# Decay exponents with their column part as the bias of ScalarE, and a norm per group in two steps, in a fused forward pass of two blocks

## What is computed

```
a_cs = cumsum(dt * A)                      # inside a block of 128 tokens
Wd   = CB * where(tri, exp(a_cs[l] - a_cs[s]), 0)
y_diag = Wd @ (x * dt)                     # dt of token s
y    = y_fwd + y_bwd + d_skip * x
y    = y * silu(z)
yg   = yg * rsqrt(mean(yg * yg) + eps)     # a group: 4 heads, 256 channels
```

## Time and profile before

| | |
|---|---|
| median of 3 runs | 2742.26 us (2741.68 to 2743.11) |
| profiled execution | 2741.83 us, its span 2739.7 us |
| busy share of the span | PE 97%, PEld 79%, DVE 53%, ACT 42%, POOL 5% |
| DMA | 225.5 MB, mean 82 GB/s |
| granted TensorE clock, mean | 0.983 |
| stage of the change | about 1390 to 1965 us of the span |

### The profile page before, as it was taken

How to read it: one execution, slowest core, us unless ns; L and a number is a source line. 1 busy time by engine, 2 the same in 40 slices (tenths; PEclk the granted TensorE clock), 3 DMA queues, 4 the chain that set the end, 5 groups by cost and what they waited for, 6 DMA issues and landing times.

```text
span 2739.7 us, 32829 instructions
## 1 busy us (share of the span) xinstructions
PE 2650.5 (97%) x13058; PEld 2171.1 (79%) x13058; DVE 1452.2 (53%) x2317; ACT 1141.4 (42%) x1888; POOL 143.8 (5%) x144
## 2 busy tenths in 40 slices
PE   7999999999899999999899999999989999999998
PEld 5888778888676778888678998888867887788886
DVE  5554453433556454333568776675565356443343
ACT  5253443322456543322464655554244334442232
POOL 1110000000100010000001010000000000000000
PEclk9999999999999999999989999999989999999999
DMA  4212223742222123233222121112211243222321
GB/s 138 66 56 69 69 77 100 137 131 95 92 76 83 62 73 105 93 93 107 66 76 68 52 68 54 47 62 77 80 39 39 67 142 108 77 93 93 100 100 62
DMA packets 201112, 225.52 MB, mean 82 GB/s; under 512 B 25152, under 2 KB 133984, under 8 KB 200704
## 3 DMA queue, kind: packets, MB, share of 16 engines
q1 hardware_dynamic: 200960, 223.43, 27.1%
HBM read 213.96 MB, written 9.44 MB: 82 GB/s over the span
## 4 chain that ended last, share of the span: by engine, by line
PE 87%; DVE 6%; ACT 4%; issue 2%; DMA 0%; POOL 0%; SPq 0%; DVEq 0%; POOLq 0%; ACTq 0%
PE bank L1771 22%; PE bank L1773 22%; PE bank L1772 22%; PE bank L1777 2%; PE bank L1778 2%; PE bank L1779 2%; PE bank L1789 2%; PE bank L1985 1%; PE bank L1806 1%; PE bank L1966 1%; PE bank L1950 1%; PE bank L1949 1%; ACT whi L2032 1%; PE bank L1940 1%; PE bank L1922 1%
## 5 line engine op out<-in xcount | busy, mean ns | idle before, releaser
L2240 DVE TENSOR_TENSOR wlo<-raw,whi 128x1024 fp32r<-128x1024 f32 (+1 forms) x389 | 488.6, 1261 | 739.0 <-ACT whi L2032 736.8
L2032 ACT ACTIVATE whi<-raw 128x1024 fp32r<-128x1024 f32 (+1 forms) x389 | 406.9, 1053 | 662.7 <-PE bank L1773 621.3
L1771 PE MATMUL bank<-XAh,whi 128*128 128x512 f32 x1536 | 620.8, 404 | 19.0 <-DVE XAl L2248 10.9
L1772 PE MATMUL bank<-XAl,whi 128*128 128x512 f32 x1536 | 605.3, 394 | 0.0
L1773 PE MATMUL bank<-XAh,wlo 128*128 128x512 f32 x1536 | 604.9, 394 | 0.0
L1771 PEld LDWEIGHTS bank<-XAh,whi 128*128 128x128 f32 x1536 | 292.7, 191 | 97.1 <-issue 31.6
L1773 PEld LDWEIGHTS bank<-XAh,wlo 128*128 128x128 f32 x1536 | 292.3, 190 | 63.1
L1772 PEld LDWEIGHTS bank<-XAl,whi 128*128 128x128 f32 x1536 | 292.9, 191 | 58.9 <-issue 0.7
L1771 PE MATMUL bank<-XBh,whi 128*128 128x512 f32 x816 | 324.8, 398 | 1.7 <-DVE XBl L2246 1.7
L1773 PE MATMUL bank<-XBh,wlo 128*128 128x512 f32 x816 | 318.1, 390 | 0.0
L1772 PE MATMUL bank<-XBl,whi 128*128 128x512 f32 x816 | 317.8, 389 | 0.0
(11 more groups left out here) (331 smaller groups left out, 3599.6 us busy)
## 6 DMA issues: line engine op xcount, KB each, us to landing
raw<-in_w_in SPq DMA_DIRECT2D x68, 512.0 KB, 3.7
raw<-in_up SPq DMA_DIRECT2D x64, 512.0 KB, 3.7
raw<-in_down SPq DMA_DIRECT2D x64, 512.0 KB, 3.7
raw<-in_a_w_in SPq DMA_DIRECT2D x32, 512.0 KB, 4.1
raw<-in_w_up SPq DMA_DIRECT2D x32, 512.0 KB, 3.6
raw<-in_w_down SPq DMA_DIRECT2D x32, 512.0 KB, 3.2
raw<-in_w_kv SPq DMA_DIRECT2D x16, 512.0 KB, 3.5
raw<-in_w_ssd_branch SPq DMA_DIRECT2D x16, 512.0 KB, 3.4
```

Source lines behind the costliest of these rows:

```text
L1771: pe.matmul(out, wh[:, w, c], xh[:, x, 0:s.ntok], start=st, stop=False)
L1772: pe.matmul(out, wh[:, w, c], xl[:, x, 0:s.ntok], start=False, stop=False)
L2032: act.activation(s.hi, s.raw, ACT.Copy).then_inc(s.whi[0], 1)
L2240: dve.tensor_tensor(s.lo, s.raw, s.hi.bitcast(F32), ALU.subtract).then_inc(s.wlo[0], 1)
```

## The change

- sc_arg: the eight matmuls L1940 of a head are gone; the two L1938 stay.
- sc_exp: the Relu of a direction becomes four, one for each token block of 128 columns, whose bias is a column of a new tile K.room (128 partitions x 256): 80 + cs - ln dt, for that block, direction and head. The Exp stays.
- dt_chain: the two dt_rows steps and the two row_parts for rowT[2], rowT[3] are gone, with their distances of two pieces each. L2448, a DVE tensor_tensor, becomes one scalar_tensor_tensor that writes K.room. rowT has 2 tensors, not 4.
- sc_norm now ends with the four Squares; one of the two waits for them on ACT's own queue is gone. A new step sc_scale, one piece later, has the table load, Ln, Exp and the four scalings. sc_back comes four pieces after that.

```diff
-            for d in range(2):
-                yield from p.spaced(2)
...
-                s3 = add("dt_rows", bank=b, ln=t0, d=d, rows=s2.rows, mm=sig("dt.rowmm"))
-                last = split_rows(rowT[2 + d], b, s3.mm, t1, t2, last)
...
-            s7 = add("sc_norm", Y=Y.t, q=q, ss=ss, gated=gates[1], zn=sig("sc.zn"))
+            s7 = add("sc_norm", Y=Y.t, q=q, ss=ss, gated=gates[1], before=ready.get("zn", NONE), means=sig("sc.means"))
...
-            q.free(s7.zn)
+            q.free(s7.means)
+            yield
+            yield from p.spaced(1)
+            s7 = add("sc_scale", Y=Y.t, ss=ss, means=s7.means, zn=sig("sc.zn"))
+            ready["zn"] = s7.zn
             yield
             yield from p.spaced(4)
...
-                pe.matmul(b.t[:, :], one, s.rowT[d][:, :], start=True, stop=False)
-                for c in range(4):
-                    m = pe.matmul(b.t[:, c * P:(c + 1) * P], s.rowT[2 + d][:, c * P:(c + 1) * P], one, start=False, stop=c == 3)
-                m.then_inc(s.arg[d][0], 1)
+                pe.matmul(b.t[:, :], one, s.rowT[d][:, :], start=True, stop=True).then_inc(s.arg[d][0], 1)
...
-                act.activation(s.E.t[:, d, :], s.banks[d].t[:, :], ACT.Relu, scale=-1.0, bias=cap).then_inc(s.below[d][0], 1)
+                for c in range(4):
+                    x, n = slice(c * P, (c + 1) * P), c * 64 + 32 * d + s.hd
+                    m = act.activation(s.E.t[:, d, x], s.banks[d].t[:, x], ACT.Relu, scale=-1.0, bias=K.room[:, n:n + 1])
+                m.then_inc(s.below[d][0], 1)
...
-            dve.tensor_tensor(s.ln.t[:, 0:256], s.ln.t[:, 0:256], cs, ALU.subtract).then_inc(s.rows[0], 1)
+            dve.scalar_tensor_tensor(out=K.room[:, :], in0=cs, scalar=CAP, in1=s.ln.t[:, 0:256], op0=ALU.add, op1=ALU.subtract).then_inc(s.cols[0], 1)
```

More of the change, by code:

```diff
@@ L1193, in make_plan @@
         ss = sb("sst", [P, 8], scope=sc)
-        rowT = [sb(f"rowT{i}", [96, S], F32R, scope=sc) for i in range(4)]
-        K.cap = sb("cap", [P, 1], scope=sc)
+        rowT = [sb(f"rowT{i}", [96, S], F32R, scope=sc) for i in range(2)]
+        K.cap, K.room = sb("cap", [P, 1], scope=sc), sb("room", [P, 256], scope=sc)
         pick = K.pick = sb("pick", [96, 32], F32R, scope=sc)
@@ L1211, in dt_chain @@
             s2 = add("dt_sums", dts=dts, banks=bs, adt_done=s1.adt_done, ln=t0, sums=sig("dt.sums"), ln_in=sig("dt.lnin"), ln_out=sig("dt.lnout"),
-                     cum=sig("dt.cum"), tail=sig("dt.tail"), exps=sig("dt.exps"), done=sig("dt.done"), rows=sig("dt.rows"))
+                     cum=sig("dt.cum"), tail=sig("dt.tail"), exps=sig("dt.exps"), done=sig("dt.done"), cols=sig("dt.cols"))
             bs[0].free(s2.tail)
@@ L1219, in dt_chain @@
             yield
-            for d in range(2):
-                yield from p.spaced(2)
-                while not three.room(1):
-                    yield WAIT
-                b = three.take()
-                s3 = add("dt_rows", bank=b, ln=t0, d=d, rows=s2.rows, mm=sig("dt.rowmm"))
-                last = split_rows(rowT[2 + d], b, s3.mm, t1, t2, last)
-                yield
-            e0.free(last)
+            e0.free(last, s2.cols)
             e1.free(last)
-            ready["dt"], ready["rows"] = s2.done, last
+            ready["dt"], ready["rows"], ready["cols"] = s2.done, last, s2.cols
         def split_rows(dst, bank, mm, t1, t2, before=NONE):
@@ L1375, in outputs @@
                     s = add("sc_arg", banks=bs, rowT=rowT, hd=4 * g + r_, rows=ready["rows"], arg=[sig("sc.arg"), sig("sc.arg")])
-                    s = add("sc_exp", banks=bs, E=E, arg=s.arg, below=[sig("sc.below"), sig("sc.below")], exp=[sig("sc.exp"), sig("sc.exp")])
+                    s = add("sc_exp", banks=bs, E=E, hd=4 * g + r_, cols=ready["cols"], arg=s.arg, below=[sig("sc.below"), sig("sc.below")], exp=[sig("sc.exp"), sig("sc.exp")])
                     for b, v in zip(bs, s.below):
@@ L1885, in pe_program @@
             m.then_inc(s.sums[0], 1)
-        elif k == "dt_rows":
-            on.wait_ge(*s.rows)
-            on.room(s.bank)
-            for c in range(4):
-                for x in (0, 32, 64):
-                    m = pe.matmul(s.bank.t[x:x + 32, c * P:(c + 1) * P], s.ln.t[:, c * 64 + 32 * s.d:c * 64 + 32 * s.d + 32], K.ident, start=True, stop=True)
-            m.then_inc(s.mm[0], 1)
         elif k == "sc_tr":
@@ L2168, in act_program @@
             cap = K.cap[:, 0:1]
+            on.wait_ge(*s.cols)
             for d in range(2):
                 on.wait_ge(*s.arg[d])
-                act.activation(s.E.t[:, d, :], s.banks[d].t[:, :], ACT.Relu, scale=-1.0, bias=cap).then_inc(s.below[d][0], 1)
+                for c in range(4):
+                    x, n = slice(c * P, (c + 1) * P), c * 64 + 32 * d + s.hd
+                    m = act.activation(s.E.t[:, d, x], s.banks[d].t[:, x], ACT.Relu, scale=-1.0, bias=K.room[:, n:n + 1])
+                m.then_inc(s.below[d][0], 1)
             for d in range(2):
@@ L2179, in act_program @@
             for c in range(4):
-                m = act.activation(s.q.t[:, (c % 2) * 256:(c % 2) * 256 + 256], Y[:, c, :], ACT.Square, accum_out=ss[:, c:c + 1]).then_inc(*on.link())
-                if c % 2:
+                m = act.activation(s.q.t[:, (c % 2) * 256:(c % 2) * 256 + 256], Y[:, c, :], ACT.Square, accum_out=ss[:, c:c + 1])
+                m.then_inc(*((s.means[0], 1) if c == 3 else on.link()))
+                if c == 1:
                     on.linked()
+        elif k == "sc_scale":
+            ss, Y = s.ss, s.Y
+            on.linked()
+            on.wait_ge(*s.means)
             need("natural_log_exp_and_others")
```

## The result

The changed kernel takes 2694.25 us (median; 2693.83 to 2697.15) against 2742.69 us (2741.68 to 2743.16): a ratio of 0.983, with a 95% interval of 0.981 to 0.984. Its profiled execution took 2694.49 us, 47.3 less than the 2741.83 of the kernel before. The direction held, and so did the two terms of work saved (the matmuls and the start of the stage); the loss of 10 us did not come, and the norm gave about twice its term.

The account below looks back on a forecast made before the run. PE was taken to bound the kernel (busy 2650.5 of 2739.7 us), except at the stage's start. Matmuls -26.7, start -8, loop +10 and norm -5 gave -29.7 from 2741.83, so 2712 us; range 2699 to 2727.

Parts of the forecast that it names:

- PE loses eight matmuls a head: In sc_arg on PE: each head saves 0.83 us, 32 heads 26.7 us; bounds 23.7 and 27.5.
- The start of the stage: Without two dt_rows and two row_parts, PE's waits of 4.56 and 4.00 us shrink: 8 us saved, bounds 3 and 12.
- the lower price: For sc_arg's small matmuls: the skill's about 81 ns each, making the 256 matmuls worth 20.7 us.
- ACT gains six instructions a head: Relus in sc_exp: eight of 128 columns at 0.31 us add 1.35 us a head, 43 us of ACT.
- The line through 512 and 256 columns: Price of a 128-column ACT activation, from 512-column Relus (0.57 us) and 256-column scalings (about 0.40): 0.32 us.
- What is late next, +10 us: In x tiles DVE falls behind ACT, slack runs out, PE waits in five to seven groups: +10 us, bounds 0 and 31.
- all is absorbed: Rival for the whole program: no new waits and the old ones go, 2700 us; chance 0.13.
- The norm in two steps, -5 us: At sc_norm on ACT: the tap runs 3.4 us sooner, two PE waits with dips cost some 8 us; -5 counted.
- A dip of the clock: PE at 1.2 GHz instead of 2.4 behind a wait, for eight or nine matmuls: some 1.8 us.
- The loop's bound of 0: Lower bound of the loss from ACT and DVE taking turns in x tiles: 0 us, all absorbed.
- the norm's -8: Largest gain allowed for splitting sc_norm into two steps: 8 us, the two PE waits with their dips.

Follow-up runs that it names:

- e5: The changed kernel with the two dt_rows and their row_parts put back, writing to a tensor nobody reads; 2703.95 us, ratio 0.986.
- e7: The changed kernel with each Exp cut into four of 128 columns and Relus of 64 columns, 14 more ACT instructions a head; 2726.39 us, ratio 0.994.
- e6: The changed kernel with each Exp of 512 columns cut into four of 128, six more ACT instructions a head; 2700.13 us, ratio 0.984.
- e3: The changed kernel with sc_back three pieces after sc_scale instead of four, so a group's cycle is 12 pieces again; 2695.44 us, ratio 0.983.
- e2: The kernel before with nothing changed but the norm in two steps; 2731.54 us, ratio 0.9966.
- e1: The changed kernel with sc_norm left in one step, so only the bias part of the change; 2705.47 us, ratio 0.987.
- e4: The changed kernel with the norm in one step and sc_back five pieces after it, keeping the cycle of 13 pieces; 2706.2 us, ratio 0.987.
- e10: The changed kernel with each remaining row_parts cut into two steps and three pieces between the two row_parts instead of one; 2689.53 us, ratio 0.981.

## Why the forecast was off, and where it held

- **PE loses eight matmuls a head: right.** 26.6 us for 26.7; a sc_arg of 0.47 us, with nothing between it and the next step. The 128-column matmuls were worth what the rows said, not the 20.7 us of the lower price.
- **The start of the stage: right in the sum, not in its parts.** 8.2 us between the marks and 6 to 9 in e5 for 8. The wait of 4.56 us went whole, for the 3.8 of it that were counted, and the one of 4.00 fell to 0.6, for 2. What the forecast missed is the second row_parts, which remains: the split behind it comes no sooner, and without the matmuls of dt_rows PE stands 2.55 us in front of it, where below 1.5 was expected. With the dip behind L1914, which went too (1.7 us behind the mark), the start comes to 9.9.
- **ACT gains six instructions a head: mis-sized.** +0.92 us a head from the first Relu to the end of the Exps, not +1.35. Over the 32 heads it is 28.3 us of ACT (80.1 to 108.4), not 43. The line through 512 and 256 columns took its second point from scalings, 0.40 apart, that read and write SBUF, while the Relus read PSUM. The runs show a difference between the two: the Exps of 128 columns within SBUF follow each other after 0.29 us (in e7 eight of them begin at 1547.57 and what is behind them at 1549.91), near the forecast's 0.31, and the Relus after 0.25. Whether it is the source or the function that makes the 0.04 us was not tried. A Relu of 128 columns lasts 0.389 us by itself (the group of 256 of them in the changed kernel, below), so the overlap is 0.14. The Trainium skill, "ScalarE: Activation LUTs", section What ACT_TABLE_LOAD costs, has 280 + 0.833 x 128 = 387 ns for the single one, with which the trace agrees, and 93 ns of overlap, with which the Relus don't; the 294 ns from start to start that the two figures make agree with the Exps.

```profile
L2160 ACT ACTIVATE E<-bank,room 128x128 f32<-128x128 f32 x256 | 69.4, 389 | 19.0 <-PE bank L1927 18.9
```

- **What is late next, +10 us: the step that failed.** The mis-sized price is not the reason, or a small part of it: e6, with 1.1 us a head over the changed kernel, so 2.0 over the kernel before and more than the 1.35 assumed, lost 2 to 5 us. What failed is the step from "both come close to nothing at the end of a group's x tiles" to "1 to 2 us of waiting in each of five to seven groups". The first half came true for E, whose 4.9 us of slack became 0.5 (nine heads have 1.0 or less), and not for the split for z, whose 4.1 us became 3.0 (ready at 1585.51, used at 1588.51). The second half took for granted that the lag of four periods goes on beyond the slack. It does not: in e3 DVE's lag is never over 1.6 us, it does not grow from tile to tile, and at the next group's first x tile it is gone. What is left of the slack decides, and PE waits 1.1 us in all, of which e2 has 0.9 as well. The loss begins with e6, where ACT is busy for 70% of the stretch, and is steep by e7, at 74%; the forecast had 10 us of it at 67%, and the changed kernel is at 63%. The rival "all is absorbed" had the outcome, at a chance of 0.13, though of the slack of 4.9 us that it named only 0.5 was left over.
- **The norm in two steps, -5 us: right in its mechanism, half its size.** e2 measured 9.6 us, and with the bias it is 10.0 from e1 to e3 and 10.8 from e4 to e3, all on one chip. Two errors. A dip of the clock was priced at 1.8 us, from eight or nine matmuls; that is right for the three dips at the start (3.40 us at half the clock each, 1.7 lost) and too little for these two (2.9 and 3.4). Such a price had to be read behind the waits in question. And "the loaded ACT gives some back" did not happen; more waiting would have been there without the split (6.4 us in e1 for 4.4), and it removes that too. That the number of table loads stays was wrong by two (37 before, 35 after), which costs nothing that can be seen: e3 has 37 and the same time. Group 4's norm on ACT in the changed kernel (against the earlier trace rows) shows how the split of the norm takes PE's wait away:

```profile
1653.12 1.04 ACT L2018 ACTIVATE whi<-raw 128x1024 fp32r<-128x1024 f32 x1
...
1654.70 1.28 ACT L2009 ACT_TABLE_LOAD   x1
...
1656.56 1.71 ACT L2184 ACTIVATE Y<-Y,sst 128x256 f32<-128x256 f32 x4
1658.17 0.76 ACT L2137 ACTIVATE CV<-bank,convh 128x512 f32<-128x512 f32 x1
```

The block from the table load to the tap is as long as ever, 3.47 us. But the split of the next weights now runs ahead of it, at 1653.12, and no longer behind it and the tap.

- **The sum.** Against -29.7: the loop's +10 that did not come, 4.6 more for the waits of the norm and their dips (3.3 and 6.3 for 5), and 1.9 more for the start with its dip (9.9 for 8), so 16.5 of the 17.6 us that separate -29.7 from -47.3; 1.1 us are not placed. The range left out the case in which all is absorbed and the norm is worth double. The loop's bound of 0 was there, but the norm's -8 was too small for what it held.

## What to carry to other kernels

Slack is spent over a whole group of pieces, not in one period: before charging a loss for an engine that falls behind, add up the lag over the pieces that also give it back, and set the remainder against the slack at the instruction that would wait, for every such instruction and not for one. Afterwards read the slack again: a kernel that shows no new wait can stand 0.5 us from one, as this one does. Where an in-order queue holds a block that waits or runs for 3 us (a norm, a split that bounces between two engines), cut it at the point where another engine answers and let other pieces in between: twice here, that shortened PE's waits (4.4 us to 0.9 in e2, 2.5 and 0.6 to 1.4 at the start of e10). To a PE wait of a microsecond or more add a bound for the clock that may fall behind it: here from nothing to 3.4 us.

## What the runs showed of the hardware

- In the kernel before, PE was busy for 6.80 us at half the clock behind a wait of 1.03 us, and for 5.70 behind one of 3.33, so the shorter wait cost up to 4.4 us with its dip. But the length of a wait does not tell whether a dip follows: a wait of 1.26 us in e4 and one of 2.03 in e7 have none, as these stretches show, e4's first, nor have the 1.1 of e3 and the 1.4 of e10, while the 2.5 of the changed kernel has one of 3.40 us. e6 has 5.5 us of waits in 400 us, none over 1.04, and the clock at 1.00 throughout. What decides was not tried.

```profile
1750.00:1800.00 50.00, 48.74 (x266) 41.83 (x265) 38.45 (x56) 28.60 (x64) 4.09 (x2) 1.00 0.25 74
1500.00:1550.00 50.00, 47.97 (x286) 42.41 (x284) 37.01 (x56) 42.46 (x134) 5.82 (x3) 1.00 0.22 64
```

- Activations of 128 columns from PSUM with a bias from memory follow each other after 0.25 us (eight in 2.00), those of 64 columns after 0.20 (sixteen from 1544.43 to 1547.57 in e7, 3.14 us). Cutting one of 512 columns (0.57) into four costs 0.43 us, into eight 1.0. The three distances lie on one line, 0.14 us and 0.83 ns a column (an estimate from 0.57, 0.25 and 0.20). Exps of 128 columns within SBUF, with a bias from memory too, follow each other after 0.29 us.
